# Handing the merged branches to the output projection one tile at a time, in a three-stack transformer kernel in fp32

## The reference, cut to what matters

```python
h = modulate(rms_norm_2(x, g), shift, scale)
z = h @ w_in                    # p, u, v, q, k, v, and three gates of D_MODEL columns each
y = sigmoid(gate_0) * (pool_mix(...)   @ w_pool_out)
y = y + sigmoid(gate_1) * (sgu_mix(...)    @ w_sgu_out)
y = y + sigmoid(gate_2) * (attention(...)  @ w_attn_out)
x = x + g_mod * (y @ w_o)       # w_o is 1024 x 1024
...
x = x + g_mod * ffn(modulate(rms_norm_2(x, g2), shift2, scale2))
```

## Time and profile before

| | |
|---|---|
| median of 3 runs | 2229.2 us (2219.29 to 2231.6) |
| the profiled execution | 2227.24 us |
| its span | 2225.5 us |
| TensorE busy | 2057.1 us, 92% of the span |
| VectorE busy | 1099.4 us, 49% |
| ScalarE busy | 867.6 us, 39% |
| TensorE's mean granted clock | 0.959 of full |

### The profile page before, as it was taken

The page is one execution under the profiler, slowest core; times in us unless marked ns, Lnnn a source line. Parts: engine busy times, 40 slices in busy tenths (PEclk is TensorE's granted clock), DMA queues, the critical chain, the costliest instruction groups (busy, mean ns, idle before and its releaser), DMA issues.

```text
span 2225.5 us, 34272 instructions
## 1 busy us (share of the span) xinstructions
PE 2057.1 (92%) x14744; PEld 1818.3 (82%) x14744; DVE 1099.4 (49%) x1683; ACT 867.6 (39%) x1221; POOL 166.0 (7%) x165
## 2 busy tenths in 40 slices
PE   5889899999898999699999989999999798989998
PEld 4769899989698999578688877777777687988997
DVE  4464544455455555623534355444444525556554
ACT  4364533343645434422622234222222425444442
POOL 0030100002200000301430000000000003000000
PEclk8899999999998999789999999999999999999999
DMA  5345387754643555512543323444544320654553
GB/s 162 107 155 168 107 212 195 201 167 154 226 152 95 178 182 171 139 57 74 164 121 102 108 78 127 157 153 152 169 134 151 125 75 26 184 166 149 174 172 113
DMA packets 326933, 317.09 MB, mean 142 GB/s; under 512 B 12901, under 2 KB 311660, under 8 KB 326526
## 3 DMA queue, kind: packets, MB, share of 16 engines
q1 hardware_dynamic: 318976, 293.89, 42.7%
q0 software_dynamic: 3904, 12.03, 2.6%
q10 hardware_dynamic: 3902, 8.98, 1.1%
HBM read 306.01 MB, written 8.85 MB: 141 GB/s over the span
## 4 chain that ended last, share of the span: by engine, by line
PE 75%; DVE 9%; DMA 8%; ACT 5%; issue 1%; POOL 0%; SPq 0%; ACTq 0%; DVEq 0%; POOLq 0%
PE acc L602 20%; PE acc L603 19%; PE acc L604 19%; DVE w_low L1625 5%; ACT w_high L1200 4%; DMA raw<-in_l_w_up 2%; PE pss L759 2%; PE acc L617 1%; PE pst L770 1%; DMA raw<-in_l_w_down 1%; PE acc L618 1%; DMA raw<-in_w_mod 1%; PE acc L619 1%; DVE normed L1641 1%; DMA raw<-in_w_attn_out 1%
## 5 line engine op out<-in xcount | busy, mean ns | idle before, releaser
L1625 DVE TENSOR_TENSOR w_low<-raw,w_high 128x2048 fp32r<-128x2048 f32 (+3 forms) x252 | 539.8, 2143 | 433.1 <-ACT w_high L1200 432.7
L602 PE MATMUL acc<-normed,w_high 128*128 128x256 f32 (+2 forms) x2080 | 664.8, 320 | 18.1 <-DVE w_low L1625 17.1
L603 PE MATMUL acc<-normed,w_high 128*128 128x256 f32 (+2 forms) x2080 | 656.3, 316 | 0.0
L604 PE MATMUL acc<-normed,w_low 128*128 128x256 f32 (+2 forms) x2080 | 656.0, 315 | 0.0
L1200 ACT ACTIVATE w_high<-raw 128x2048 fp32r<-128x2048 f32 (+3 forms) x252 | 447.2, 1775 | 406.3 <-PE acc L604 297.0
L602 PEld LDWEIGHTS acc<-normed,w_high 128*128 128x128 f32 (+1 forms) x2080 | 400.6, 193 | 52.2 <-DVE w_low L1625 22.9
L603 PEld LDWEIGHTS acc<-normed,w_high 128*128 128x128 f32 (+1 forms) x2080 | 400.9, 193 | 23.0
L604 PEld LDWEIGHTS acc<-normed,w_low 128*128 128x128 f32 (+1 forms) x2080 | 400.5, 193 | 23.5
L602 PE MATMUL acc<-inner,w_high 128*128 128x256 f32 (+2 forms) x1160 | 367.2, 317 | 4.8 <-DVE inner L1638 2.4
L603 PE MATMUL acc<-inner,w_high 128*128 128x256 f32 (+2 forms) x1160 | 364.2, 314 | 0.0
L604 PE MATMUL acc<-inner,w_low 128*128 128x256 f32 (+2 forms) x1160 | 363.7, 314 | 0.0
(11 more groups left out here) (196 smaller groups left out, 2142.5 us busy)
## 6 DMA issues: line engine op xcount, KB each, us to landing
raw<-in_w_ff SPq DMA_DIRECT2D x64, 1024.0 KB, 5.5
raw<-in_w_mod SPq DMA_DIRECT2D x48, 1024.0 KB, 5.2
raw<-in_w_in SPq DMA_DIRECT2D x48, 512.0 KB, 3.8
raw<-in_l_w_gate SPq DMA_DIRECT2D x22, 1024.0 KB, 5.7
raw<-in_l_w_up SPq DMA_DIRECT2D x22, 1024.0 KB, 6.0
raw<-in_w_in SPq DMA_DIRECT2D x18, 1024.0 KB, 5.2
raw<-in_l_w_down SPq DMA_DIRECT2D x16, 1024.0 KB, 6.6
raw<-in_l_w_qkv SPq DMA_DIRECT2D x12, 1024.0 KB, 5.2
```

Source lines behind the costliest of these rows:

```text
L602: mm(dst, lh, rh, start=i == 0, stop=False)
L603: mm(dst, lh, rl, start=False, stop=False)
L604: ins = mm(dst, ll, rh, start=False, stop=i == n - 1)
L1625: V.tensor_tensor(WL[:, s % NSPLIT, 0:nw], RAW[:, slot_of[u], 0:nw], WH[:, s % NSPLIT, 0:nw].bitcast(F32), ALU.subtract).then_inc(w_low, 1)
```

## The change

The last branch now hands tile k on as soon as it is summed. ACT makes the high half straight from `y_t` (`merged_high`), DVE the low half from `y_t` and the high half (`merged_low`); the copy to `TMP` is gone. The first n = 2048 / T tiles (4 in layer 0, all 8 in layer 1) go to words 2048 and up of `inner`, the others to `normed` as before. `merge_turns` says which tiles a turn m hands on: tile m-1 in turn m; in layer 0 that is tiles 0 to 3 in turns 1 to 4, and tiles 4 to 7 in turn 7, since `normed` is read by the gates up to then; in layer 1 tiles 0 to 5 in turns 1 to 6, and tiles 6 and 7 in turn 7. The product with `w_o` reads through `merged(T)` and waits tile by tile, now with 8 counts in both layers. The sum in the last branch no longer waits for its own end (`link`), but counts `val_done`; the products of a turn go to alternate halves of `TMP`.

```diff
+        def merged(T):
+            n = 2048 // T
+            a = hr(2048, n, T)
+            return Pair(Rows(a.high, AT[:, 0], n), Rows(a.low, AT[:, 1], n))
...
+        def merge_turns(T):
+            n = 2048 // T
+            turns = {m: [m - 1] if 0 < m <= n else [] for m in range(KD)}
+            turns[KD - 1] = list(range(min(n, KD - 2), KD))
+            return turns
...
-                ready = by_tile(T)
-                project(4, at_pair, T, ready=ready)
+                base = st["store"]
+                st["store"] += KD
+                project(4, merged(T), T, ready=lambda k: base + k + 1)
...
+            def merged_high(T, k):
+                st["store"] += 1
+                st["val"] += 1
+                act.wait_ge(val_done, st["val"])
+                nc.scalar.activation(merged(T).high[:, k, 0:T], y_t(T)[:, k, :], ACT.Copy).then_inc(high_done, 1)
...
+                        if b3 == 2:
+                            for k in merge_turns(T)[m]:
+                                merged_high(T, k)
                         split()
-                highs(norm_chunks(T))
...
+            def merged_low(T, k):
+                st["store"] += 1
+                dve.wait_ge(high_done, st["store"])
+                d = merged(T)
+                V.tensor_tensor(d.low[:, k, 0:T], y_t(T)[:, k, :], d.high[:, k, 0:T].bitcast(F32), ALU.subtract)\
+                    .then_inc(stored, 1)
...
-                        tmp = TMP[:, 0, 0:T]
+                        tmp = TMP[:, m % 2, 0:T]
+                        if b3 == 2 and T > S:
+                            for k in merge_turns(T)[m]:
+                                if k < KD - 1:
+                                    merged_low(T, k)
                         V.tensor_tensor(tmp if b3 else y, SM[:, i % 2, 0:T], b[:, 0:T], ALU.mult).then_inc(free, 1)
                         if b3:
                             own(free)
-                            link(V.tensor_tensor(y, y, tmp, ALU.add))
+                            ins = V.tensor_tensor(y, y, tmp, ALU.add)
+                            if b3 == 2:
+                                ins.then_inc(val_done, 1)
+                            else:
+                                link(ins)
+                        if b3 == 2:
+                            for k in merge_turns(T)[m]:
+                                if T == S or k == KD - 1:
+                                    merged_low(T, k)
                         split()
-
-                k = 0
-                for d in norm_chunks(T):
-                    n = d.high.shape[1]
-                    i = room()
-                    V.tensor_copy(tmp_like(i, d.high), y_t(T)[:, k:k + n, :]).then_inc(val_done, 1)
-                    k += n
-                    pending.append((i, d, None))
-                flush()
```

More of the change, by code:

```diff
@@ L216, in tiles, with __init__, __getitem__ @@
                 return Pair(self.high[:, lo:hi, :], self.low[:, lo:hi, :])
+        class Rows:
+            def __init__(self, first, rest, n):
+                self.first, self.rest, self.n = first, rest, n
+            def __getitem__(self, at):
+                p, k, c = at
+                return self.first[p, k, c] if k < self.n else self.rest[p, k, c]
+        def merged(T):
+            n = 2048 // T
+            a = hr(2048, n, T)
+            return Pair(Rows(a.high, AT[:, 0], n), Rows(a.low, AT[:, 1], n))
         def hr(base, tiles, T):
```

## The result

| | before | changed |
|---|---|---|
| median of 6 runs each | 2227.52 us (2219.29 to 2231.6) | 2209.79 us (2203.74 to 2215.68) |
| ratio, 95% interval | | 0.9924 (0.9898 to 0.995) |
| the profiled execution, its span | 2227.24, 2225.5 us | 2215.68, 2213.9 us |
| TensorE's mean granted clock | 0.959 | 0.961 |

The change makes the kernel faster by 0.76%, some 17 us (0.5% to 1.0%). Measured once more beside the kernel before, the ratio was 0.9918 (0.9895 to 0.994).

A forecast was written before the change was run, and what follows sets the result against it. TensorE's standing still or running slowly was taken as the bound. Gains of 8.67 (layer 0) and 8.48 us (layer 1), 17.15 together, took 2227.24 to 2210.1, or 2212 at the median; own range 2206 to 2218, full range 2204 to 2221.

The forecast's parts named there:

- What bounds: Whole kernel: TensorE bounds it; pauses before `w_o` (6.27 and 6.49 us idle) cost twice, through slow steps behind them.
- Layer 0's sum: Layer 0, last branch to w_o 1: pause 6.43 us plus slow steps 2.24, together 8.67 us gained.
- Three low halves by 1288.9: Layer 0, turn 7: VectorE's low halves of tiles 4 to 6 end by 1288.9, delaying the product from 1288.44.
- The 0.33 us that stays: Layer 1, ahead of `w_o`: TensorE ready at 1977.32 starts at about 1977.65, so 0.33 us of pause remains.
- The prices of the halves: Last branch: 0.64 us on ACT, 0.70 on DVE a tile in layer 0; 0.41 and 0.42 in layer 1; hidden.
- the 0.2 us that I had worked out as VectorE's margin: Layer 1's last branch: halves fit into DVE's idle time of at least 0.70 us ahead of `w_low`, by 0.2 us.
- (a): Rival, layer 1: its weights become the wait, typically 2 to 4 us lost, 2214 to 2219; costly half chance 0.07.
- Its two signs: Layer 1: TensorE waits for `w_low` in branch 2, or at w_o 1; no size given.
- (b): Rival, later stages: queue-paced loads give back one layer's gain, 8.5 us, giving 2221; chance 0.06.
- (c): Rival, behind the two places: uninterrupted work brings a long lower clock, slower, some 2241 us; chance 0.03.
- (d): Rival, both layers: TensorE still waits for tile 7 or late counts, 1 to 2 us each; within forecast's 0.84.
- The clock's part: Layer 0, behind the pause: slow steps 2.24 us; by the skill's varying counts 1.2 to 2.8.

The follow-up runs named there:

- the filled pause: Kernel before, with unread matmuls (28 in layer 0, 54 in layer 1) between the last branch product and the first of `w_o`: 2215.02 us, ratio 0.999.
- layer 0 alone: Changed kernel with layer 1's copies, 5 chunks and `highs` as before, behind the split of w_o 1: 2205.78 us, ratio 0.995.
- the table of four traces: Kernel before and changed kernel, each traced twice, nothing else changed; between the two places 668.76 to 671.75 us; second measurement 2218.8 and 2202.69 us.
- the changed order: Kernel before with only the split of w_o 1 moved behind the handing on of the merged tiles: 2210.93 us, ratio 0.9965.
- before again: Kernel before, unchanged, run once more for a second trace: 2218.8 us.

## Why the prediction was right

- **What bounds.** The pauses and the slow steps behind them were the whole of the gain. Shown: the two stretches fell by 8.67 and 8.48 us, the very sums of the prediction, and the filled pause separated their two parts, 4.3 us for the clock and 12.8 for standing still. That both agree to a hundredth is luck: with the second traces the gain is 8.94 and 7.4 us.
- **Layer 0's sum** was right, with one step of its working wrong. "Three low halves by 1288.9" overlooked the wait for the product's bank ahead of them. They ran behind TensorE's last matmul, the product of turn 7 came 1.4 us later than I had it, tile 7 was in hand by 4.6 us and not 6, and `w_low` of w_o 1 by 2.6 (1299.37 against 1301.98) and not 3.8. It would have cost something only where these margins are smaller.
- **Layer 1.** The 0.33 us that stays was 0.24 in one trace and 0.59 in the other (0.36 and 0.71 from start to start, less a step). w_o 1 was split by 1977.28 + 2.29 = 1979.57 and wanted at 1979.94: 0.37 us in hand, 0.2 predicted.
- **The prices of the halves** were right: 0.63 and 0.69 us at 512 tokens, 0.41 and 0.42 at 256, and so was that the idle time covers them; the idle time ahead of `w_low` fell from 0.70 to 0.29 us. Three times as many halves cost nothing, so the 0.2 us that I had worked out as VectorE's margin wasn't its end.
- **The rivals.** (a), the weights of layer 1: not with three times the work. Its two signs did appear, once each and small: TensorE waited 0.22 us for `w_low` within the last branch in the first trace of the changed kernel, and 0.43 us for w_o 0 in the second. Both follow late loads, and the kernel before has such steps too (one of 0.33 us in its second trace). (b), given back by later loads: layer 0 alone and the table of four traces speak against it. (c), a lower clock for working through: the granted clock is 1.00 throughout both places and in the 20 us behind each, up to the next norm. (d): the tiles never come late.
- **The clock's part.** The slow steps cost 2.24 us in one trace of before and 2.51 in the other, in layer 0 (11 and 12 of them), and 2.16 and 2.24 in layer 1, but 1.46 there in the kernel that has only layer 0 changed (22, 23 and 14). The Trainium skill (TensorE: Matmul & The Clock Gate, Part 1) has the count of slow matmuls, at a kernel's start, vary from run to run. The runs agree that it varies, behind a pause too.
- **The span.** The prediction's 2210.1 us for a profiled execution was missed by 5.6, in stages that have nothing to do with the change; the medians, 2212 predicted and 2209.79 measured, are closer than the scatter gives a right to expect.

## What to carry to other kernels

Where an engine stands still at a hand-over, list what stands in the helping engines' queues between the last input and the first output: here work for later (a split wanted 10 us on) stood ahead of work for now, and all inputs but the last had long been there. Moving only that later work costs it elsewhere; passing on what is ready ahead of both the last input and the later work gave nearly all. When whole-run times scatter by 10 us, compare the stretch between two landmarks of TensorE in each trace: it repeated to 0.3 us where only the kernel's own waits were in it, and to 1.3 us where a load's landing and the number of slow steps came in. And before buying back the clock, ask what TensorE will wait for once it is fast.

## What the runs showed of the hardware that I had not expected

- A pause of 2.65 us from start to start left the granted clock at 1.00, one of 3.90 us was followed by 0.50; both in one trace of the kernel with the changed order. Two cases give no rule, and the length of the pause isn't all: ahead of the first norm's tiles the changed kernel's TensorE was idle for 1.09 and 1.57 us, with eight small matmuls between, and 0.50 followed as well.
- Matmuls whose result nobody reads keep the clock at 1.00, both large fp32r ones on data and 128 x 128 fp32 ones on the identity, and in the long pauses at no cost that the stretches show.
- One kernel's executions reach the same instruction up to 15 us apart (1276.27 and 1290.87). All of it in the kernel before, and 8.8 of the 14.6 us in the changed one, arises between VectorE's root reciprocals near 265 and 480, in the first block's layer 0: 216.9 and 207.6 us in the two traces of before, 220.6 and 211.9 in those of the changed kernel. TensorE's longest waits in 265 to 490 (engine, line, what for: us in total, times, longest), before and before again:

```profile
PE acc L602 <- DVE w_low L1625: 10.4, 6, 3.0
```

```profile
PE acc L602 <- DVE w_low L1625: 4.8, 6, 1.7
```

and in the same stretch of the first, ACT waits 21.6 us for the loads of `w_down` and 12.4 for those of `w_up`, in the second 15.9 and 3.7. So TensorE's waits for split weights differ by 5.6 us there, and those waits are behind loads that land at different times. In the changed kernel's two traces TensorE's waits are 14.0 and 6.2 us in that stretch, but ScalarE's waits for `w_down` go the other way (18.0 and 25.4). That the loads make the scatter is likely and not shown, and why they land so differently stays open.
